# Attention steps over both kv groups: score and value products that alternate between the halves of the array

## What is computed

```
s = einsum('bnqkgd,bnskd->bnkgqs', qb, kb) * HEAD_DIM ** -0.5     # blocks of 128 queries, 256 keys (128 in block 0)
s = where(valid, s - slopes * dist, -inf)
m = maximum(max(s), sink);  p = exp(s - m);  denom = sum(p) + exp(sink - m)
o = einsum('bnkgqs,bnskd->bnqkgd', p / denom, vb)
```

## Time and profile before

| | |
|---|---|
| median of 3 runs | 1454.22 us (1453.82 to 1455.38) |
| profiled execution | 1454.27 us |
| its span (first to last instruction) | 1452.4 us |
| PE busy | 1380.9 us, 95% of the span |
| DVE, ACT, POOL busy | 58%, 40%, 21% |
| mean granted clock of TensorE | 0.973 |

### The profile page before, as it was taken

The page is one execution under the profiler, slowest core; times in us unless marked ns, Lnnn a source line. Parts: engine busy times, 40 slices in busy tenths (PEclk is TensorE's granted clock), DMA queues, the critical chain, the costliest instruction groups (busy, mean ns, idle before and its releaser), DMA issues.

```text
span 1452.4 us, 27604 instructions
## 1 busy us (share of the span) xinstructions
PE 1380.9 (95%) x10588; PEld 1347.9 (93%) x10588; DVE 840.9 (58%) x1287; ACT 579.8 (40%) x1110; POOL 301.7 (21%) x397
## 2 busy tenths in 40 slices
PE   8999996999999999978999999989699999999995
PEld 8988896999999999967999999989699999999995
DVE  6457438665555622258777777753865555562224
ACT  5344335433333322235556655643543333332221
POOL 2123124211111100033222222212421111120002
PEclk9989998999999999987999999999899999999998
DMA  7311220222222322221222222213022222233201
GB/s 268 106 44 44 74 88 29 88 87 88 87 88 88 111 98 84 79 86 45 89 88 88 88 88 74 89 46 102 30 88 88 86 88 90 91 108 110 86 34 62
DMA packets 38526, 123.32 MB, mean 85 GB/s; under 512 B 4104, under 2 KB 9864, under 8 KB 38344
## 3 DMA queue, kind: packets, MB, share of 16 engines
q1 hardware_dynamic: 34248, 111.92, 24.0%
q10 hardware_dynamic: 4048, 10.20, 1.9%
q0 software_dynamic: 176, 0.44, 0.1%
HBM read 113.98 MB, written 8.57 MB: 84 GB/s over the span
## 4 chain that ended last, share of the span: by engine, by line
PE 83%; DVE 10%; issue 3%; ACT 2%; DMA 0%; ACTq 0%; DVEq 0%; SPq 0%; POOL 0%
PE acc L379 72%; PE aux L591 2%; DVE x L1260 2%; DVE w_lo L1059 1%; DVE mix L1255 1%; PE aux L633 1%; PE aux L481 1%; PE acc L397 1%; PE aux L501 1%; DVE lev L1357 1%; DVE h_lo L1067 1%; DVE scratch L1460 1%; PE aux L605 1%; DVE lev L1351 1%; PE aux L423 1%
## 5 line engine op out<-in xcount | busy, mean ns | idle before, releaser
L1059 DVE TENSOR_TENSOR w_lo<-raw,w_hi 128x512 fp32r<-128x512 f32 (+1 forms) x372 | 315.8, 852 | 398.7 <-ACT w_hi L707 398.2
L379 PE MATMUL acc<-h_hi,w_hi 128*128 128x272 f32 x2208 | 474.5, 297 | 37.0 <-DVE h_lo L1067 32.9
L379 PE MATMUL acc<-h_hi,w_lo 128*128 128x272 f32 x2208 | 463.3, 292 | 0.0
L379 PE MATMUL acc<-h_lo,w_hi 128*128 128x272 f32 x2208 | 462.7, 292 | 0.0
L379 PEld LDWEIGHTS acc<-h_hi,w_hi 128*128 128x128 f32 x2208 | 354.1, 192 | 47.2 <-issue 27.6
L707 ACT CAST w_hi<-raw 128x512 fp32r<-128x512 f32 (+1 forms) x372 | 238.4, 643 | 380.0 <-PE acc L379 375.5
L379 PEld LDWEIGHTS acc<-h_lo,w_hi 128*128 128x128 f32 x2208 | 354.5, 193 | 0.0
L379 PEld LDWEIGHTS acc<-h_hi,w_lo 128*128 128x128 f32 x2208 | 351.9, 192 | 0.0
L379 PE MATMUL acc<-g_hi,w_lo 128*128 128x272 f32 x684 | 141.7, 289 | 0.0
L379 PE MATMUL acc<-g_hi,w_hi 128*128 128x272 f32 x684 | 141.4, 288 | 0.0
L379 PE MATMUL acc<-g_lo,w_hi 128*128 128x272 f32 x684 | 141.0, 288 | 0.0
(11 more groups left out here) (247 smaller groups left out, 1615.3 us busy)
## 6 DMA issues: line engine op xcount, KB each, us to landing
raw<-in_w_up SPq DMA_DIRECT2D x88, 512.0 KB, 3.5
raw<-in_w_down SPq DMA_DIRECT2D x32, 704.0 KB, 4.0
raw<-in_w_in_c SPq DMA_DIRECT2D x32, 512.0 KB, 3.5
raw<-in_w_in_ab SPq DMA_DIRECT2D x18, 512.0 KB, 3.7
raw<-in_w_out_ab SPq DMA_DIRECT2D x8, 512.0 KB, 3.4
S<-in_state ACTq DMA_DIRECT2D x8, 512.0 KB, 4.2
o_ss<-Snew ACTq DMA_DIRECT2D x8, 512.0 KB, 2.6
raw<-in_w_out_c SPq DMA_DIRECT2D x8, 512.0 KB, 3.5
```

What stands on the lines that cost most here:

```text
L379: mm = pe.matmul(acc[out][:, t, 0:H], w[slot][:, cols], mv[:, kk_, t * H:(t + 1) * H], start=start and k == 0 and q == 0, stop=stop and k ...
L1059: dve.tensor_tensor(w_lo[n % 2][:, to], raw[n % 4][:, cols], w_hi[n % 2][:, to], ALU.subtract).then_inc(lo_ready, 1)
```

## The change

A step becomes block n = s // 2 and a pair of heads of both kv groups, pair = s % 2: heads 2 pair and 2 pair + 1 of group 0 and of group 1. The scores of group g go to bank A[g]; the matmuls alternate between partitions 0 to 63 and 64 to 127 (rows of the array). In the value product the two groups alternate between output partitions 0 to 63 and 64 to 127 (columns of the array), 256 moving columns each instead of 512. The copy to y_hi and the subtraction to y_lo read 128 partitions x 256 instead of 64 x 512. Bias slices and sinks are picked to match; the sinks are reordered on the host. Counts of matmuls: scores 4 a step as before; value product 4 a step instead of 2 (2 instead of 1 in block 0). Waits and the order between the halves stay.

```diff
             def scores(s):
-                n, g = divmod(s, 2)
+                n, pair = divmod(s, 2)
                 lo_k = WIN if n == 0 else 0
-                rows = slice(64 * g, 64 * g + 64)
                 pe.wait_ge(s_biased, 2 * s + 2)
-                for j in range(GRP):
-                    mm = pe.matmul(A[j // 2][:, (j % 2) * 256 + lo_k:(j % 2) * 256 + 256],
-                                   q_sb[rows, j, n * WIN:(n + 1) * WIN],
-                                   k_sb[rows, (n - 1) * WIN + lo_k:(n + 1) * WIN], start=True, stop=True)
+                for j in range(2):
+                    for g in range(2):
+                        rows = slice(64 * g, 64 * g + 64)
+                        mm = pe.matmul(A[g][:, j * 256 + lo_k:j * 256 + 256],
+                                       q_sb[rows, 2 * pair + j, n * WIN:(n + 1) * WIN],
+                                       k_sb[rows, (n - 1) * WIN + lo_k:(n + 1) * WIN], start=True, stop=True)
                 mm.then_inc(s_done, 1)
...
             def attention_out(s):
-                n, g = divmod(s, 2)
+                n = s // 2
                 pe.wait_ge(pT_copied, 2 * s + 4)
                 first = 1 if n == 0 else 0
                 for c in range(first, 2):
-                    mm = pe.matmul(A[2][64 * g:64 * g + 64, :], vtok[:, n - 1 + c, 64 * g:64 * g + 64], pT[:, c, :],
-                                   start=c == first, stop=c == 1)
+                    for g in range(2):
+                        rows = slice(64 * g, 64 * g + 64)
+                        mm = pe.matmul(A[2][rows, 0:256], vtok[:, n - 1 + c, rows], pT[:, c, 256 * g:256 * g + 256],
+                                       start=c == first, stop=c == 1)
                 mm.then_inc(o_done, 1)
...
-                n, g = divmod(s, 2)
-                r = slice(64 * g, 64 * g + 64)
-                act.copy(y_hi[r, 0:GRP, n * WIN:(n + 1) * WIN], A[2][r, :].rearrange("p (j q) -> p j q", j=GRP)
-                         ).then_inc(yb_hi, 1)
+                n, pair = divmod(s, 2)
+                act.copy(y_hi[:, 2 * pair:2 * pair + 2, n * WIN:(n + 1) * WIN],
+                         A[2][:, 0:256].rearrange("p (j q) -> p j q", j=2)).then_inc(yb_hi, 1)
...
                     for a in range(2):
-                        dve.tensor_tensor(pr[g][:, 2 * a:2 * a + 2, w],
+                        dve.tensor_tensor(pr[pair][:, 2 * a:2 * a + 2, w],
                                           A[a][:].rearrange("p (j k) -> p j k", j=2)[:, :, w],
-                                          bias[:, 4 * g + 2 * a:4 * g + 2 * a + 2, w], ALU.add).then_inc(s_biased, 1)
-                    view, sink = pr[g][:, :, w], vec[:, V_SINK + 4 * g:V_SINK + 4 * g + 4]
-                    z = sm[:, g]
+                                          bias[:, 4 * a + 2 * pair:4 * a + 2 * pair + 2, w], ALU.add
+                                          ).then_inc(s_biased, 1)
+                    view, sink = pr[pair][:, :, w], vec[:, V_SINK + 4 * pair:V_SINK + 4 * pair + 4]
+                    z = sm[:, pair]
...
-                n, g = divmod(s, 2)
-                r, c = slice(64 * g, 64 * g + 64), slice(n * WIN, (n + 1) * WIN)
-                dve.tensor_tensor(y_lo[r, 0:GRP, c], A[2][r, :].rearrange("p (j q) -> p j q", j=GRP),
-                                  y_hi[r, 0:GRP, c], ALU.subtract).then_inc(yb_lo, 1)
+                n, pair = divmod(s, 2)
+                j, c = slice(2 * pair, 2 * pair + 2), slice(n * WIN, (n + 1) * WIN)
+                dve.tensor_tensor(y_lo[:, j, c], A[2][:, 0:256].rearrange("p (j q) -> p j q", j=2),
+                                  y_hi[:, j, c], ALU.subtract).then_inc(yb_lo, 1)
```

More of the change, by code:

```diff
@@ L1137, in softmax_in @@
                 else:
-                    g = s % 2
+                    pair = s % 2
                     w = slice(WIN, 2 * WIN) if s < 2 else slice(0, 2 * WIN)
@@ L1756, in _layouts @@
         + [cols(f["hgrn_lb_logits"][l]) for l in range(2)] + [cols(f["hgrn_norm_g"][0])]
-        + [np.broadcast_to(sinks, (P, 8)), sinks[4 * (row // 16 % 2) + row // 4 % 4][:, None]], 1)
+        + [np.broadcast_to(sinks.reshape(2, 2, 2).transpose(1, 0, 2).reshape(8), (P, 8)), sinks[4 * (row // 16 % 2) + row // 4 % 4][:, None]], 1)
     d["st_a"] = f["state_conv_a"][0].reshape(NB, 2, CA, P).transpose(3, 2, 0, 1)
```

## The result

The changed kernel took 1444.5 us (median of 4 runs, 1442.75 to 1447.06) beside 1454.8 us for the kernel before (1453.82 to 1455.9): ratio 0.9926, 95% interval 0.9912 to 0.994, so 8.7 to 12.8 us faster. Forecast were 1445.9 us and 8.4 us. Its profiled execution took 1442.98 us with a span of 1441.1, which is 11.3 us under the span before. Three microseconds more than forecast in that one execution are to be explained; run again later, the same kernel gave 1446.68.

A forecast was written before the change was run, and what follows sets the result against it. TensorE, busy 95% of the span, bounds it, with the loop through y_lo close behind. Gains of 3.77 us up to transposes(2), 3.77 to transposes(7) and 0.86 behind sum to 8.4: 1454.3 becomes 1445.9 us; 8-in-10 range 1441.8 to 1450.0.

The forecast's parts named there:

- TensorE's terms: Attention steps: both halves overlap, so streaming halves; full scores save 0.83 us, full value products 0.86, 12.3 us in all.
- Rivals (2): Attention matmuls: only column halves overlap, row halves don't, so only value products gain; 4.7 us saved, 1449.6 us; chance 0.10.
- (4): Attention matmuls: order has no effect and none overlap, only the shorter y_lo counts; 1453.7 us; chance 0.06.
- rival (5): Scores and value steps: each of 44 changes of half costs 0.28 us; 12.3 us more, 1466.6 us; chance 0.05.
- Rival (1): Scores and value steps: a matmul's two records stay in line, 5 rounds for 8 records; 6.6 us saved, 1447.7 us; chance 0.08.
- The loop: Transposes(2) to (7): ScalarE, GpSimd and VectorE, ending in y_lo, hold TensorE in four of five rounds; gain 3.77 us.
- Rival (3): Attention rounds: the loop doesn't hold TensorE, so all 12.3 us and the 0.74 gap come; 1441.3 us; chance 0.06.
- The clock: Half-clock stretch at scores 1 and the projection behind: up to 2.0 us gained or lost, in the range, not the sum.
- My price of a change of shape: Sample products alternating between 128 and 4 rows: 0.28 us of each 0.33 us matmul goes into the change of shape.

The follow-up runs named there:

- the snake: Kernel before, sample value products reordered: for odd samples the 4-row matmul goes first, 8 changes of shape instead of 15; 1454.51 us. Same edit on the changed kernel: 1445.81 us.

## Why the prediction was right

**TensorE's terms.** Scores 1.09 and value product 1.00 were forecast, 1.06 and 1.01 measured; 0.67 and 0.57 became 0.65 and 0.58; scores 1 saved 0.84 for 0.83. That row halves overlap like column halves, which rested on the nearest row only, is so. That row is the sample scores. Their records under way in 30 ns, from 53.20 us of the kernel before, show the overlap of column groups directly: four have started within 0.04 us, where scores of one half start 0.22 us apart or more.

```profile
L454 PE MATMUL aux<-kc,qbd x4: 300/300/301, 53.2 to 53.2; 128*32 128x132 f32 x4
```

That the two halves write different banks, my other reason, wasn't tried apart: the value products of both halves write one bank and took 1.01 us for 1.86. The sum charged nothing for a change of half, and none shows: scores with three changes in a step took 1.06 us, with one 1.07. Rivals (2), (4) and (5) fall with that.

**Rival (1)**, a matmul that can't be overtaken, falls as well: 8 records in 4 pairs, not in 5 rounds, and with grouped orders still 4. The two records under way at the start of the grouped scores, 0.013 us apart, speak against it for the halves, as the sample scores' 0.59 us did for column groups. The argument that neighbours must differ was mine, and it was wrong.

**The loop.** Forecast were rounds of 10.11, 10.07, 9.17, 10.11, 10.07; measured 9.98, 9.96, 9.18, 9.98, 9.96. The links were named rightly. The small excess of 0.13 and 0.11 is around y_lo, which was costed by its length alone (0.69 to 0.42). VectorE's timeline of the kernel before has, on either side of the y_lo at 143.20:

```profile
142.92 0.25 DVE L1080 SCALAR_TENSOR_TENSOR scratch<-sp,vec,scratch 128x32 f32<-128x32 f32 x1
...
143.92 1.29 DVE L1143 TENSOR_TENSOR pr<-aux,bias 128x512 f32<-128x512 f32 x2
```

There y_lo starts 0.03 us behind the end of the operation before it, and the next one starts 0.03 behind its own end. After the change both overlap: y_lo starts at 133.41, where L1082 ends at 133.49, and the next starts at 133.75, where y_lo ends at 133.83. The first 0.1 shortens the rounds that end with transposes(3) and (6), the second those that end with (4) and (7). The waits I listed ahead of (3), (4), (6), (7) as 0.8 to 1.0 us came as 0.68, 0.60, 0.66 and 1.68: a wait also costs 0.19 in the transposes behind it (1.06 for 0.87 in the chain), and ahead of (7) I forgot that TensorE, with no scores to do, arrives earlier. The intervals, on which the sum rests, don't depend on that. Rival (3) is out: TensorE waits.

**The clock.** It was put at 0, with 2.0 us either way, and gave 2.5 in the profiled execution. That is the term that was mis-sized: it looked only at the projection behind scores 1 (which gave 0.80), and 1.65 us came from the sample products ahead of it. It varies with the execution, so that the first profile lies 11.3 us under the kernel before is in part luck. In comparisons of medians the gain was 10.3 us at first, and later 8.6 and 9.9, against two medians of the kernel before next to it; the forecast of 8.4 lies just below them: under the first interval (8.7 to 12.8), inside the later one (0.9923 to 0.995, 7.3 to 11.2).

**My price of a change of shape**, 0.28 us, on which rival (5) rested, was too high: I had charged all of a small matmul's time beyond its streaming to the change. Only 0.11 is the change's; 0.27 per matmul stays with the snake (4.39 us over 16). With it rival (5) would have been 4.8 us of cost and not 12.3.

## What to carry to other kernels

In this kernel two float32 matmuls that use different halves of the array, by rows (into two banks) or by columns, ran at the same time (1.92 to 1.06 us, 1.86 to 1.01 us), so the work of a step should be cut such that both halves have some; how it is ordered inside the step didn't matter (1.07 and 1.02 us with both orders grouped). Before counting what the busiest engine saves, follow the loop that returns to it through the others: here it kept back 3.5 of the 7.7 us that TensorE saved between transposes(2) and (7), and 2.75 of them came back by moving two things in their queues, a subtraction of 0.4 us ahead of a split that takes 2.39 us and ends 0.55 us behind GpSimd's normalising, and the exponentials ahead of a copy. And where an effect is below 0.5% (nine executions of the changed kernel span 6.5 us of 1445), read it from like stretches of the profiles, with the clock beside them, before believing a median of four, or its interval.

## What was not expected of the hardware

- A record that stands four places behind in program order starts with the first when it is for the other half: with grouped scores two start 0.013 us apart, and the step takes 1.07 us, the alternating one 1.06, while 8 records of one half take 1.92.
- Two kernels with the same attention to a tenth of a microsecond differ by 5 us in single executions (1448.03 and 1442.98), with a granted clock of 0.95 and 0.97 in the same 360 us. Two runs of one kernel had medians of 1448.42 and 1443.73.
- VectorE's split of 0.69 us took 2.38 or 2.39 beside four of GpSimd's normalisings in the changed kernel (it starts at 100.22, 111.95, 129.34 and 141.07, they at 100.17, 111.50, 129.28 and 140.62), and ended 0.55 us behind each. Not beside all: a split from 120.34 took 0.69, and the normalising from 120.33 took 2.45. The y_lo of the convolution also took longer once it fell in the split's place (0.70 became 2.39 in the kernel with y_lo first and the exponentials early, where a normalising of 1.89 us starts at 139.27):

```profile
139.35 2.39 DVE L1225 TENSOR_TENSOR y_lo<-scratch,y_hi 128x544 fp32r<-128x544 f32 x1 [0.16 <-ACT y_hi L825]
```
